# Products that nothing reads, on TensorE ahead of four stages of an encoder layer

## The reference

```python
x = x + jnp.concatenate([y_hy, y_rw, y_na], axis=-1) @ w_out[l]
h = rmsnorm(x, norm2_g[l]).reshape(Bn * L, D_MODEL)
x = x + hier_moe(h, moe_wg[l], moe_bg[l], moe_we[l], moe_be[l],
                 moe_w1[l], moe_w3[l], moe_w2[l]).reshape(Bn, L, D_MODEL)
...
# in hier_moe: best group of 4, top 2 of its 8 experts, and for each block of tokens
yb = (jax.nn.silu(xb @ w1[e]) * (xb @ w3[e])) @ w2[e]
...
return rmsnorm(x, norm_f_g)
```

## Time and profile before

| | us |
|---|---|
| median of 3 runs (lowest, highest) | 1920.58 (1918.44, 1923.24) |
| the profiled execution, its own time | 1916.2 |
| its span | 1914.4 |
| TensorE busy | 1693.2 |

### The profile page before, as it was taken

The page is one execution under the profiler, slowest core; times in us unless marked ns, Lnnn a source line. Parts: engine busy times, 40 slices in busy tenths (PEclk is TensorE's granted clock), DMA queues, the critical chain, the costliest instruction groups (busy, mean ns, idle before and its releaser), DMA issues. The chain is left out here.

```text
span 1914.4 us, 41843 instructions
## 1 busy us (share of the span) xinstructions
PE 1693.2 (88%) x17234; PEld 1275.1 (67%) x17234; DVE 1136.5 (59%) x1943; ACT 847.1 (44%) x1334; POOL 271.8 (14%) x353
## 2 busy tenths in 40 slices
PE   5999999988885999898893798699999999999984
PEld 4777777866653777787772687466666666666652
DVE  5568888726764544454346555566565665656754
ACT  5256666413221444343341311465565655656533
POOL 0020000011210433343233000100000000000003
PEclk8999999999997899999996798799999999999997
DMA  5225445341101111111502215699898998998927
GB/s 169 82 77 149 119 130 152 123 155 66 67 22 62 59 59 60 57 59 58 214 13 89 85 67 213 230 367 377 358 375 360 360 377 359 376 369 350 392 92 275
DMA packets 99350, 355.26 MB, mean 186 GB/s; under 512 B 16663, under 2 KB 55959, under 8 KB 84600
## 3 DMA queue, kind: packets, MB, share of 16 engines
q1 hardware_dynamic: 86520, 306.83, 43.1%
q0 software_dynamic: 8064, 29.36, 3.9%
q10 hardware_dynamic: 4608, 16.78, 2.1%
HBM read 294.75 MB, written 56.10 MB: 183 GB/s over the span
## 5 line engine op out<-in xcount | busy, mean ns | idle before, releaser
L2284 DVE TENSOR_TENSOR e_rl<-proj,e_rh 128x1024 fp32r<-128x1024 f32 x256 | 304.6, 1222 | 145.3 <-ACT e_rh L2220 144.4
L2220 ACT ACTIVATE e_rh<-proj 128x1024 fp32r<-128x1024 f32 x256 | 258.8, 1054 | 49.6 <-PE e_ph L51 30.4
L51 PE MATMUL e_ph<-e_rh,e_xh 128*128 128x512 f32 x512 | 220.8, 431 | 16.6 <-DVE e_rl L2284 14.0
L2201 PE MATMUL e_py<-mix,proj 128*128 128x512 f32 x512 | 225.0, 592 | 0.7 <-issue 0.7
L51 PE MATMUL e_ph<-e_rh,e_xl 128*128 128x512 f32 x512 | 201.7, 394 | 0.0
L51 PE MATMUL e_ph<-e_rl,e_xh 128*128 128x512 f32 x512 | 200.9, 392 | 0.0
L51 PE MATMUL a_b<-a_xh,a_wh 128*128 128x512 f32 x432 | 177.7, 411 | 5.8 <-DVE a_wl L587 3.3
L2201 PEld LDWEIGHTS e_py<-mix,proj 128*128 128x128 f32 x512 | 97.1, 190 | 110.7 <-issue 108.1
L51 PE MATMUL a_b<-a_xh,a_wl 128*128 128x512 f32 x432 | 170.1, 394 | 0.0
L51 PE MATMUL a_b<-a_xl,a_wh 128*128 128x512 f32 x432 | 169.9, 393 | 0.0
L51 PEld LDWEIGHTS e_ph<-e_rh,e_xh 128*128 128x128 f32 x512 | 97.4, 190 | 47.3 <-DVE e_rl L2284 19.7
(11 more groups left out here) (377 smaller groups left out, 3237.2 us busy)
## 6 DMA issues: line engine op xcount, KB each, us to landing
proj<-in_moe_w SPq DMA_DIRECT2D x64, 2048.0 KB, 14.2
mix<-in_moe_w SPq DMA_DIRECT2D x32, 2048.0 KB, 8.5
proj<-scan_operands SPq DMA_DIRECT2D x64, 320.0 KB, 4.2
expert_rows<-e_yo ACTq DMA_DIRECT2D x32, 512.0 KB, 11.1
scan_operands<-late SPq DMA_DIRECT2D x56, 256.0 KB, 2.6
proj<-in_w_in SPq DMA_DIRECT2D x27, 512.0 KB, 4.2
proj<-in_x SPq DMA_DIRECT2D x16, 512.0 KB, 6.1
expert_rows<-proj SPq DMA_DIRECT2D x1, 7680.0 KB, 25.1
```

Source lines behind the costliest of these rows:

```text
L51: m = e.matmul(out, lhs[a], rhs[b], start=first and n == 0, stop=last and n == 2)
L2201: m = e.matmul(py[h][:, :], at[:, k, :], w2[j][:, k, h * HALF:(h + 1) * HALF], start=(k == 0), stop=(k == KF - 1))
L2220: e.activation(rh[s % RING][:, :], piece(j, s), ACT.Copy).then_inc(high, 1)
L2284: e.tensor_tensor(rl[s % RING][:, :], piece(j, s), rh[s % RING][:, :].bitcast(F32), ALU.subtract).then_inc(low, 1)
```

## The change

A helper `keep_clock(e, S, bank, n)` issues n fp32 products of 128 columns, of the identity with the identity, into a PSUM bank that the next real products overwrite. They wait for no semaphore, and release none. It is called five times, at four places: 16 ahead of `project_tile(0)`, 16 between `tokens_of_blocks(6)` and `ranks(7)`, 32 ahead of `turn(0, 0)` and 8 behind it, 48 ahead of the loop of the final sum.

```diff
+def keep_clock(e, S, bank, n):
+
+
+    for _ in range(n):
+        e.matmul(bank[:, 0:P], S.ident[:, :], S.ident[:, :], start=True, stop=True)
...
+                keep_clock(e, S, acc[1][0], 16)
                 project_tile(0)
                 for t in range(NT):
                     b = t % 2
...
                 ranks(NT - 2)
                 tokens_of_blocks(NT - 2)
+                keep_clock(e, S, acc[0][0], 16)
                 ranks(NT - 1)
                 tokens_of_blocks(NT - 1).then_inc(ids_full, 1)
...
+                keep_clock(e, S, py[0], 32)
                 turn(0, 0)
+                keep_clock(e, S, py[0], 8)
                 e.wait_ge(x_low, 1)
                 up(0, 0, 0)
                 up(0, 0, 1)
...
             def _(e):
+                keep_clock(e, S, acc[3][:, 0, :], 48)
                 for t in range(0, NT, 2):
                     e.wait_ge(diag_ready, t // 2 + 1)
                     e.wait_ge(y_in[t], 32)
```

## The result

The changed kernel took 1933.89 us (median of 7 runs, 1929.52 to 1943.47), the kernel before 1920.04 (7 runs, 1916.85 to 1923.24) on the same chip. The ratio is 1.0077, with a 95% interval of 1.0053 to 1.0101: slower, by 14 us, and outside the range of the prediction. The profiled execution took 1934.22 us, its span is 1932.4. Ratios leave out three single executions of over 2800 us (one each of experiments 1 and 7, and one of the kernel before beside experiments 9 to 12), which the medians keep.

The account below looks back on a forecast made before the run. The prediction held that the added products could pay only through TensorE's clock, at half speed for about 4.3 us at block starts. Terms +0.1 +0.7 −0.8 +2.2 = +2.2 us gave a median of about 1922.7 us, range 1916 to 1927.

Parts of the forecast that it names:

- Place 4: 48 products ahead of the final sum: +4.4 us from holding up its rows, −2.2 given back by tile 0, sum +2.2.
- The price of a pass: Each product is two passes on TensorE, 0.22 us each at half clock and 0.112 at full; 48 products take 12.9 us.
- The mixed rival: Clock falls again at place 3 or rises late twice, or PE starts late fetching its queue: +4 to +8 us, chance 0.08.
- Places 1 to 3: Calls at the output projection, the router's end and the first expert: +0.1, +0.7 and −0.8 us.
- Place 1: 16 products ahead of the output projection, over after 5.7 us, tile 0 then at full clock: sum +0.1 us.
- Place 2: 16 products ahead of the router's last ranks: +1.8 us of delay, −1.1 given back by the block's last chain, sum +0.7.
- Place 3: 32 products ahead of the first expert's transposes, 8 behind: +2.7 us delay, −0.95 and −2.55 given back, sum −0.8.
- The rival that the products don't raise the clock: At all four places the calls stay at half clock and give nothing back: +27.6 us, 1948, chance 0.06.
- one pass a call: At all four places a product takes one record, so every call ends in time: −8.3 us, 1912, chance 0.1.
- the working: Call lengths from passes and a clock rise after 4.3 us, set against operand arrival at four places: +2.2 us, chance 0.76.

Follow-up runs that it names:

- Experiment 1: The change without the 48 products ahead of the final sum, against the kernel before: 1919.74 us, ratio 1.0004.
- experiment 7: Only 16 products ahead of the final sum, no other calls, against the kernel before: 1915.45 us, ratio 1.0003.
- experiment 9: Only the 48 products ahead of the final sum, written as a loop of 6 rounds over 8, against the kernel before: 1919.18 us, ratio 1.0006.
- experiment 12: experiment 8 with 16 products of 128 columns for the 8 wide ones ahead of the final sum, against the kernel before: 1910.83 us, ratio 0.9957.
- experiment 3: Only 12 products of 512 columns ahead of the final sum in place of 48 of 128, against the kernel before: 1920.07 us, ratio 1.0001.
- experiment 5: Only the 48 products ahead of the final sum and one more, gathers held until they are done, against the kernel before: 1931.92 us, ratio 1.0081.
- experiment 2: Only the 48 products ahead of the final sum, the four other calls taken out, against the kernel before: 1935.75 us, ratio 1.0088.
- experiment 4: Only 32 products ahead of the final sum, no other calls, against the kernel before: 1926.19 us, ratio 1.0045.
- experiment 11: The kernel of experiment 4 run once more, unchanged, for a second profile: one time, 1917.72 us.
- experiment 8: Calls trimmed to 8 at place 1, none at 2, 20 and 8 at 3, 8 wide at 4, against the kernel before: 1911.39 us, ratio 0.9965.
- experiment 10: Only 32 products ahead of the final sum, with the gathers held until they are done: one time, 1925.8 us.
- experiment 6: Only 48 products ahead of the first expert's transposes and 8 behind, no calls elsewhere, one execution: 1918.21 us.

## Why the prediction was wrong

**Place 4 is the step that failed.** "From 1868.9, over at 1881.8" and the sum of +2.2 behind it took the call for a matter of passes and clock alone. The price of a pass was right (at place 4 of the change, 5.07 us at 0.22 and 5.85 at 0.112 make 75 records, where 74 ran without a gap; experiments 3, 5 and 9 take 13.1 to 13.6 us for it, forecast 12.9, and experiment 3's stage grew by 2.9 against 2.2). What the step had no term for is that 48 products written out are 192 instructions that must be brought to PE. In this block, while 16 gathers of 512 KB hold the DMA engines, PE can't run them in a row, and the products take 25.1 us: +14.7 in the stage in place of +2.2. The conditions stand apart in the runs (the fifth column is when a packet of q8 started, in us from the block's start):

| run, products ahead of the final sum | records | instructions written out | gathers beside them | packet of q8 | gaps that end in "issue" | final sum, us |
|---|---|---|---|---|---|---|
| before, none | 0 | 0 | | none | no | 45.5 |
| the change, 48 | 96 | 192 | yes | 10.2 | yes | 60.25 |
| experiment 2, 48 | 96 | 192 | yes | 11.9 | yes | 59.7 |
| experiment 5, 48, gathers held | 96 | 192 | no | 9.9 | no | 58.6, gathers late |
| experiment 9, 6 x 8 in a loop | 96 | 32 | yes | none | no | 48.3 |
| experiment 3, 12 wide | 24 | 48 | yes | none | no | 48.4 |
| experiment 4, 32 | 64 | 128 | yes | 22.6 | three small, in the tiles | 53.0 |
| experiment 11, the same | 64 | 128 | yes | 22.9 | no | 44.9 |
| experiment 7, 16 | 32 | 64 | yes | none | no | 43.0 |
| experiment 12, 16 | 32 | 64 | yes | 3.3 | no | 43.1 |
| experiment 8, 8 wide | 16 | 32 | yes | 21.6 | no | 44.6 |

It is shown that 48 products written out under the gathers make the gaps, and that the same products under the gathers (experiment 9) or the same text without the gathers (experiment 5) don't. That PE waits for text in them is argued: it is what experiments 5 and 9 leave, and a packet of q8 runs near the first gap. But in experiment 2 the gap opens before the packet starts, the gaps go on for some 11 us behind it, and in experiments 8, 10, 11 and 12 a packet ran among the gathers with no gap. Those have fewer instructions written out, and in 8, 10 and 11 PE was at products of 512 columns by then, which use up some 5 instructions a microsecond (two for each record of 0.43 us) against 18 for those of 128 (two for 0.112). No run tells whether this is what sets them apart.

**The mixed rival came nearest to the cause, and priced it wrongly.** It says "PE starts a block late for fetching its longer queue: +4 to +8 us", with 0.08 together with two other cases. The loss came inside the block and not at its start, and cost some 12 us on top of the +2.2. The view that could have warned of it was at hand: the queues of DMA in part 3 of the page, 121 packets of text, and how often they fall into the gathers. Before, the last packet started just 3.6 us ahead of the block; with 480 more instructions in the program, 192 of them in this block, two packets more were due, and where they would fall had to be asked.

**Places 1 to 3 came out as forecast, in sum and nearly term by term.** Experiment 1: ratio 1.0004 [0.9993, 1.0014] for a forecast of 0.0 us, which the interval allows but doesn't single out.

- Place 1: forecast +0.1. The clock rose 3.1 us after the start and not 4.3, sooner than in any row of the prediction; the call was over after 5.0 us (5.7 forecast). DVE's first sum came 16.60 us into the block, 17.27 before: −0.7. The window of the rise, 0.85 for a rise at 1068.3:

```profile
1068.00:1069.00 1.00, 1.00 (x10) 1.00 (x10) 1.00 (x2) 1.00 (x2) 0.00 (x0) 0.85 1.10 321
```

- Place 2: forecast +1.8 and −1.1. The ranks came 6.56 us behind the token products, 4.70 before: +1.9. From there to the cast of the ids it took 2.59 us, 3.75 before: −1.2.
- Place 3: forecast +2.7 and −3.5, in sum −0.8. The call took 8.8 us (9.3 forecast), the first product of `up` started 1.1 us later into the block than before (the earlier trace rows against the timeline above), and warm. The stage was 1.4 us shorter. The clock in it was not as assumed, though: it was still up when the call began, fell about 1.1 us later and rose again at 1215.1, 4.6 us after the call's start. That the call's length comes near the forecast, made for half clock from the first product, is in part luck.

```profile
1210.50:1211.50 1.00, 1.00 (x9) 1.00 (x10) 0.00 (x0) 0.82 (x1) 0.31 (x1) 1.00 0.84 360
1211.70:1212.70 1.00, 1.00 (x7) 1.00 (x6) 0.93 (x1) 1.00 (x3) 0.69 (x2) 0.50 0.88 377
```

**The rival that the products don't raise the clock is out**: the clock rose in every long call, after 3.1 us at place 1 and 5.1 at place 4 (1872.2 to 1877.2). So is one pass a call: the trace has 240 records of the helper, 64, 80 and 96 by bank, for 120 products.

**What the working was worth** shows in experiments 8 and 12. By its prices each call was cut to end when its operand comes, and place 2, where the call would have held up the ranks by more than it gave back, was dropped; the medians fell by 7 us in both, against the +14 of the change. Their profiles agree on the experts (−3.2 and −3.6 for a forecast of −3.5) and give −2.4 at the final sum in experiment 12; place 1's −1.7 does not show in either, in a stage that scatters by 3.6 us. So the sum of −7 is met, and one of its terms is unproven.

**What stays open.** What PE waits for in the gaps, one by one. If it is text, why it comes in trickles for 11 us and more after the packet that started at 1882.0 to 1882.5, up to the end of the gathers, and not at once: the trace has no record of it. Whether the amount of text or the place of the packet decides: no run moved the packet by more than 1.7 us and kept the 48 products as they are. And ACT's wait in experiment 4, in one profile of two: that it too waited for text is argued from its time and from "remote" alone, and nothing here shows it.

## What to carry to other kernels

A product that only raises the clock cost nothing here as long as it ended before the operand that it waits beside (experiments 7 and 12); work out its length from records of the same form (two passes for a plain fp32 product, 0.22 and 0.112 us each here), and stop it there. Its instructions are a cost apart from its time: ahead of a stretch in which gathers fill the DMA engines, use few wide products or a small loop (the same time on PE, and some 16 us less in all by experiments 2, 3 and 9), and look in the profile for the packets of the instruction queue to see when text is fetched. When an engine's gaps end in "issue" with no semaphore behind them, look at that queue and at what fills the DMA engines in the same window, and test it with a loop, as in experiment 9.

## What the runs showed of the hardware

- The text of PE comes in packets of 16 KB on a DMA queue (q8), and 480 more instructions of PE made 123 packets of 121. The Trainium skill, "Runtime: NRT & Kernel Launch", section "Instruction fetch mechanics", says that text comes in blocks of 16 KiB and that crossing a boundary is mostly hidden. The trace agrees on the size, and on the hiding at place 3 (experiment 6, packet within the call, no gap) and for the packets of experiments 8, 10, 11 and 12. For 48 narrow products written out under gathers, at a share of 1.03 and 410 GB/s, some 12 us were lost, which is not hidden if the gaps are waits for text, as argued above.
- Under expert weights and two gathers, at a mean share of 0.92 and 340 GB/s, 96 narrow records ran without a gap (experiment 6); under sixteen gathers in a row, at 1.03 and 410 GB/s, they did not. Whether the kind of the traffic or its amount decides is not shown.
- Within its gaps PE still moved one or two records every 0.7 to 2 us, and the clock fell from 1.00 to 0.50 in them (1887.5), so such gaps cost the clock as well.
- The clock rose between 3.1 and 5.1 us after the start of a call of narrow fp32 products, in the same program (1065.2 to 1068.3 at place 1, 1872.2 to 1877.2 at place 4), and 5.9 us after it in experiment 12 (1866.3 to 1872.2).
